# Split chunks, norm scales and gated branches in PSUM banks, and the scalings of the residual between index sums, in a two-block transformer kernel

## The reference

```python
# first block
n = rms_norm(h, norm_mix);  h = h + token_mixers(n, ...)          # recurrence + windowed attention
    merged = sigmoid(gate_r) * y_rec + sigmoid(gate_a) * y_att;  return merged @ w_out
n = rms_norm(h, norm_mem);  mem_n = rms_norm(mem, norm_mem_kv)
h = h + memory_cross_attention(n, mem_n, ...)
n = rms_norm(h, norm_ffn);  h = h + conv_ffn(n, ...)              # (silu(conv(g)) * u) @ w_down
x = rms_norm(h, final_norm)
# second block
h = rmsnorm(x, norm_g)
q_lat, c_kv, k_rope, z_a, q_b, k_b, v_b, z_b, q_idx, k_idx, w_idx, gate_a, gate_b = split(h @ w_in)
q = rmsnorm(q_lat, g_q_lat) @ w_uq;   kv = rmsnorm(c_kv, g_kv_lat) @ w_ukv
y_a = mla_attention(...) * silu(z_a)
y_b = dsa_attention(..., top-k of relu(q_idx . k_idx) weighted by w_idx, rel_bias) * silu(z_b)
merged = sigmoid(gate_a) * (y_a @ w_o_a) + sigmoid(gate_b) * (y_b @ w_o_b)
out = rmsnorm(x + merged @ w_out, final_g)
```

## Time and profile before

| | |
|---|---|
| median of 3 runs | 1524.61 us (1521.25 to 1524.68) |
| the profiled execution | 1524.03 us, span 1522.0 us |
| mean granted clock of TensorE | 0.997 of full speed |
| busy share of the span | PE 95%, PEld 75%, VectorE 68%, GpSimd 55%, ScalarE 30% |
| chain that ended last, by engine | PE 76%, DVE 14%, issue 4%, ACT 3%, POOL 1%, PEld 1% |
| DMA | 127.64 MB read, 6.82 MB written, 88 GB/s over the span |

### The profile page before, as it was taken

How to read it: one execution, slowest core, us unless ns; L and a number is a source line. 1 busy time by engine, 2 the same in 40 slices (tenths; PEclk the granted TensorE clock), 3 DMA queues, 4 the chain that set the end, 5 groups by cost and what they waited for, 6 DMA issues and landing times.

```text
span 1522.0 us, 19925 instructions
## 1 busy us (share of the span) xinstructions
PE 1451.7 (95%) x6948; PEld 1138.0 (75%) x6948; DVE 1035.3 (68%) x1879; ACT 455.3 (30%) x886; POOL 838.7 (55%) x675
## 2 busy tenths in 40 slices
PE   4999999999998899999999999999899999999998
PEld 3777777776777788687888888887677777667886
DVE  6557798687259531588999995335977897686255
ACT  4555441466123111321010101102243334364111
POOL 3534323443565777266777776766645443444663
PEclk9999999999999999999999999999999999999999
DMA  5221111211332333132333333333333531322331
GB/s 204 70 70 42 42 42 49 63 56 56 114 94 84 111 110 103 51 97 84 97 97 97 97 97 99 109 102 128 85 123 98 104 87 47 118 75 99 109 96 57
DMA packets 37018, 135.61 MB, mean 89 GB/s; under 512 B 4296, under 2 KB 4552, under 8 KB 36296
## 3 DMA queue, kind: packets, MB, share of 16 engines
q1 hardware_dynamic: 33264, 121.13, 26.1%
q10 hardware_dynamic: 3672, 13.35, 3.4%
HBM read 127.64 MB, written 6.82 MB: 88 GB/s over the span
## 4 chain that ended last, share of the span: by engine, by line
PE 76%; DVE 14%; issue 4%; ACT 3%; POOL 1%; PEld 1%; DMA 0%; PEldq 0%; ACTq 0%; DVEq 0%; POOLq 0%
PE pair L575 21%; PE pair L577 20%; PE pair L576 20%; PE pair L845 3%; PE pair L873 3%; DVE X L1828 2%; PE pair L857 2%; DVE nL L1666 1%; PE pair L775 1%; DVE rstd L1684 1%; DVE sums L1675 1%; DVE nt L1688 1%; POOL wL L530 1%; DVE lev L1837 1%; DVE hT L2206 1%
## 5 line engine op out<-in xcount | busy, mean ns | idle before, releaser
L530 POOL TENSOR_TENSOR wL<-ring,wH 128x1024 fp32r<-128x1024 f32 x223 | 551.8, 2474 | 18.6
L575 PE MATMUL pair<-nH,wH 128*128 128x512 f32 x1064 | 427.8, 402 | 16.8 <-DVE nL L1666 9.1
L577 PE MATMUL pair<-nH,wL 128*128 128x512 f32 x1064 | 415.8, 391 | 0.0
L576 PE MATMUL pair<-nL,wH 128*128 128x512 f32 x1064 | 415.8, 391 | 0.0
L527 POOL TENSOR_TENSOR tick<-tick 128x1 f32<-128x1 f32 x223 | 56.3, 252 | 645.0 <-PE pair L577 635.6
L575 PEld LDWEIGHTS pair<-nH,wH 128*128 128x128 f32 x1064 | 200.3, 188 | 82.7 <-issue 27.5
L528 POOL TENSOR_SCALAR wH<-ring 128x1024 fp32r<-128x1024 f32 x223 | 239.3, 1073 | 0.0
L577 PEld LDWEIGHTS pair<-nH,wL 128*128 128x128 f32 x1064 | 200.5, 188 | 43.1
L576 PEld LDWEIGHTS pair<-nL,wH 128*128 128x128 f32 x1064 | 200.8, 189 | 40.6 <-issue 1.6
L1513 ACT ACTIVATE sgb<-cv 128x512 f32<-128x512 f32 x22 | 13.9, 634 | 208.9 <-DVE cv L2148 208.9
L575 PE MATMUL pair<-aH,wH 128*128 128x512 f32 x176 | 69.1, 392 | 0.0
(11 more groups left out here) (386 smaller groups left out, 2677.3 us busy)
## 6 DMA issues: line engine op xcount, KB each, us to landing
ring<-stream SPq DMA_DIRECT2D x223, 512.0 KB, 3.6
gvec<-gv ACTq DMA_DIRECT2D x1, 2560.0 KB
hT<-xT SPq DMA_DIRECT2D x4, 512.0 KB, 5.7
x_d<-hT ACTq DMA_DIRECT2D x1, 2048.0 KB, 7.3
toep<-gvec ACTq DMA_DIRECT2D x8, 256.0 KB, 3.5
hT<-x_d ACTq DMA_DIRECT2D x1, 2048.0 KB, 9.6
out<-yo SPq DMA_DIRECT2D x4, 512.0 KB, 4.2
cD<-const_d ACTq DMA_DIRECT2D x1, 1345.0 KB, 5.9
```

The costliest lines, as they stand in the source:

```text
L530: pool.tensor_tensor(wL[:, r % SPL, :], ring[:, r, :], wH[:, r % SPL, :].bitcast(F32), ALU.subtract).then_inc(split_done, 1)
L575: mm(out, a[0], b[0], start=first, stop=False)
L576: mm(out, a[0], b[1], start=False, stop=False)
L577: return mm(out, a[1], b[0], start=False, stop=last)
```

## The change

Nothing that is computed changes, and nothing of what TensorE, GpSimd and SyncE compute or load. What changes is where intermediate values lie, and five places in the order.

- The chunks that are split (`nt`) lie in banks 4 and 5 for ten of the fifteen uses (83 chunks): all but the outputs of the recurrence and the four attentions, where these banks are in use. VectorE writes them there, ScalarE reads the high part's source there, and `low` has one operand in PSUM.
- The inverse deviation of the norms `memory` and `c_kv` goes into bank 2, that of `q_lat` into bank 3. The scale of the final norm (`sums2`) is copied to bank 2 by one new ScalarE instruction, and the chunks 2 to 7 of `mix2` read it there. The other norms keep `rstd`.
- In both merges the gated second branch goes into banks 2 and 3 in place of `addA` and `addD`.
- The eight scalings of the residual leave their place before the inverse of `q_lat`; three stand after index sum 0, three after index sum 1, two after index sum 2. The store of the residual on ScalarE's queue moves from before the first index score's `relu` to after the last one's.
- The sums of the norms of `q_lat` and `c_kv` are each one slot earlier on TensorE.
- The two matmuls of `relb` go to bank 7, before index scores 0 and 1, each with its copy on ScalarE.
- TensorE waits for the last split chunk of `c_kv` before the transposes of `pk` into bank 4.

```diff
+IN_BANKS = {SPLIT[n] + c for n in ("mix", "merged", "memory", "mem", "ffn", "hidden", "mix2", "q_lat", "c_kv", "merged2")
+            for c in range({"hidden": FC, "q_lat": 3, "c_kv": 2}.get(n, DC))}
...
+        def split_at(k, width=S):
+            return (bank(4 + k % 2) if k in IN_BANKS else nt[:, k % 2, :])[:, :width]
...
-            mm(bank(4)[0:8, :], relb[:, :], c_d("onehot", 0, S)[rows, :], start=True, stop=True)
-            mm(bank(5)[0:8, :TOEP - S], relb[:, :], c_d("onehot", S, TOEP)[rows, :], start=True, stop=True).then_inc(gv_done, 1)
             project("q_idx", 0, 1, n_parts, inputs="mix2")
-            project("q_idx", 1, 1, n_parts)
             norm_sum("q_lat")
-            project("small", 0, 1, n_parts)
+            project("q_idx", 1, 1, n_parts)
             norm_sum("c_kv")
+            project("small", 0, 1, n_parts)
             project("z_a", 0, 1, n_parts)
             out_of_bank(pe, FIRST["small"])
-            pe.wait_ge(gv_out, 2)
-            pe.wait_ge(std_made, NORMS.index("final") + 1)
+            pe.wait_ge(nl_made, SPLIT["c_kv"] + 2)
...
             project("z_a", 1, 1, n_parts)
+            pe.wait_ge(std_made, NORMS.index("c_kv") + 1)
+            relative_bias(0, S)
             index_scores(0)
             project("z_a", 2, 1, n_parts)
+            pe.wait_ge(gv_out, 1)
+            relative_bias(S, TOEP)
             index_scores(1)
...
-                A(dst, nt[:, k % 2, :width], ACT.Copy).then_inc(nh_made, 1)
+                A(dst, split_at(k, width), ACT.Copy).then_inc(nh_made, 1)
...
             act.wait_ge(r_made, NORMS.index("final") + 1)
+            A(bank(2), sums2[:, :], ACT.Copy).then_inc(scale_out, 1)
...
-                V.tensor_tensor(lo[:, c, :], nt[:, k % 2, :width], hi[:, c, :].bitcast(F32),
+                V.tensor_tensor(lo[:, c, :], split_at(k, width), hi[:, c, :].bitcast(F32),
                                 ALU.subtract).then_inc(nl_made, 1)
...
+            def scale_of(name):
+                return {"memory": bank(2), "q_lat": bank(3), "c_kv": bank(2)}.get(name, rstd)
...
-                V.reciprocal(rstd[:, :width], std[:, :width]).then_inc(r_made, 1)
+                V.reciprocal(scale_of(name)[:, :width], std[:, :width]).then_inc(r_made, 1)
...
-                    V.tensor_tensor(add[:, c % 2, :], src, g, ALU.mult).then_inc(free, 1)
+                    V.tensor_tensor(bank(2 + c % 2), src, g, ALU.mult).then_inc(free, 1)
                     out_of_bank(dve, FIRST[stage] + 4 * (c // 2) + 2 + c % 2)
-                    V.tensor_tensor(out, add[:, c % 2, :], mt[:, c, :], ALU.add).then_inc(nt_made, 1)
+                    V.tensor_tensor(out, bank(2 + c % 2), mt[:, c, :], ALU.add).then_inc(nt_made, 1)
...
-                                       in1=sums2[:, :], op0=ALU.mult, op1=ALU.mult).then_inc(nt_made, 1)
+                                       in1=bank(2) if c > 1 else sums2[:, :], op0=ALU.mult, op1=ALU.mult).then_inc(nt_made, 1)
...
             inverse("mix2")
-            for c in range(DC):
-                V.scalar_tensor_tensor(out=hT[:, c, :], in0=hT[:, c, :], scalar=vcol("final_norm", c), in1=rstd[:, :],
-                                       op0=ALU.mult, op1=ALU.mult).then_inc(x1_made, 1)
-            dve.wait_ge(x1_made, DC)
             inverse("q_lat")
...
             index_sum(0)
+            final_normed(range(0, 3))
             silu("z_a", [2], za)
             index_sum(1)
+            final_normed(range(3, 6))
             silu("z_a", [3], za)
             index_sum(2)
+            final_normed(range(6, DC))
```

More of the change, by code:

```diff
@@ L343, in build @@
         mnL = place("mnL", [P, DC, MEM], F32R, at=wx0 + 4 * DC * S)
-        addA = place("addA", [P, 2, S])
+        top[0] += 4 * 2 * S
         mk = place("mk", [P, DC, MEM])
@@ L419, in build @@
         assert top[0] <= b0
-        addD = place("addD", [P, 2, S], at=d0)
         mg2L = place("mg2L", [P, DC, S], F32R, at=b0)
@@ L1040, in _, with relative_bias @@
             project("c_kv", 0, 2, u_parts)
-            pe.wait_ge(ld_d, 32)
-            rows = slice(0, REL_BUCKETS)
-            mm(bank(4)[0:8, :], relb[:, :], c_d("onehot", 0, S)[rows, :], start=True, stop=True)
-            mm(bank(5)[0:8, :TOEP - S], relb[:, :], c_d("onehot", S, TOEP)[rows, :], start=True, stop=True).then_inc(gv_done, 1)
+            def relative_bias(a, b):
+                rows = slice(0, REL_BUCKETS)
+                mm(bank(7)[0:8, :b - a], relb[:, :], c_d("onehot", a, b)[rows, :], start=True, stop=True).then_inc(gv_done, 1)
             project("q_idx", 0, 1, n_parts, inputs="mix2")
+            norm_sum("q_lat")
             project("q_idx", 1, 1, n_parts)
-            norm_sum("q_lat")
+            norm_sum("c_kv")
             project("small", 0, 1, n_parts)
-            norm_sum("c_kv")
             project("z_a", 0, 1, n_parts)
             out_of_bank(pe, FIRST["small"])
-            pe.wait_ge(gv_out, 2)
-            pe.wait_ge(std_made, NORMS.index("final") + 1)
+            pe.wait_ge(nl_made, SPLIT["c_kv"] + 2)
+            pe.wait_ge(ld_d, 32)
             for i in range(ST):
@@ L1683, in inverse, with normed @@
                 dve.wait_ge(std_made, i + 1)
-                V.reciprocal(rstd[:, :width], std[:, :width]).then_inc(r_made, 1)
+                V.reciprocal(scale_of(name)[:, :width], std[:, :width]).then_inc(r_made, 1)
                 dve.wait_ge(r_made, i + 1)
-            def normed(out, x, gain, c, width=S):
-                return V.scalar_tensor_tensor(out=out, in0=x[:, c, :], scalar=vcol(gain, c), in1=rstd[:, :width],
+            def normed(name, out, x, gain, c, width=S):
+                return V.scalar_tensor_tensor(out=out, in0=x[:, c, :], scalar=vcol(gain, c), in1=scale_of(name)[:, :width],
                                               op0=ALU.mult, op1=ALU.mult)
@@ L1695, in norm @@
                     beside(c)
-                    normed(open_split(name, c, width), x, gain, c, width).then_inc(nt_made, 1)
+                    normed(name, open_split(name, c, width), x, gain, c, width).then_inc(nt_made, 1)
                     if c:
@@ L2043, in first_branch, with merge @@
                            V.tensor_tensor(mt[:, c, :], src, g, ALU.mult).then_inc(free, 1))
-            def merge(stage, sg, mt, add, name, hi, lo, beside=lambda p: None):
+            def merge(stage, sg, mt, name, hi, lo, beside=lambda p: None):
                 def use(c, src, g, free):
                     out = open_split(name, c)
-                    V.tensor_tensor(add[:, c % 2, :], src, g, ALU.mult).then_inc(free, 1)
+                    V.tensor_tensor(bank(2 + c % 2), src, g, ALU.mult).then_inc(free, 1)
                     out_of_bank(dve, FIRST[stage] + 4 * (c // 2) + 2 + c % 2)
-                    V.tensor_tensor(out, add[:, c % 2, :], mt[:, c, :], ALU.add).then_inc(nt_made, 1)
+                    V.tensor_tensor(out, bank(2 + c % 2), mt[:, c, :], ALU.add).then_inc(nt_made, 1)
                     if c:
@@ L2095, in add_memory @@
                         accumulate("memory", c, MEM)
-            merge("att_mix", sgA, mtA, addA, "merged", mgH, mgL, add_memory)
+            merge("att_mix", sgA, mtA, "merged", mgH, mgL, add_memory)
             inverse("memory", MEM)
@@ L2243, in index_sum, with final_normed @@
                                            op0=ALU.mult, op1=ALU.add).then_inc(t_acc, 1)
+            def final_normed(chunks):
+                for c in chunks:
+                    V.scalar_tensor_tensor(out=hT[:, c, :], in0=hT[:, c, :], scalar=vcol("final_norm", c), in1=rstd[:, :],
+                                           op0=ALU.mult, op1=ALU.mult).then_inc(x1_made, 1)
             index_sum(0)
+            final_normed(range(0, 3))
             silu("z_a", [2], za)
             index_sum(1)
+            final_normed(range(3, 6))
             silu("z_a", [3], za)
             index_sum(2)
+            final_normed(range(6, DC))
             dve.wait_ge(t_acc, 8)
@@ L2295, in _ @@
             barrier()
-            merge("b_mix", sgD, mtD, addD, "merged2", mg2H, mg2L)
+            merge("b_mix", sgD, mtD, "merged2", mg2H, mg2L)
             dve.wait_ge(ld_x1, 16)
```

18 lines of the change are left out of this document (11 added, 7 removed).

## The result

The changed kernel takes **1509.49 us** (median of 4 runs, 1509.26 to 1509.78) against 1524.51 us for the kernel before, measured with it: a ratio of 0.9913, with a 95% interval of 0.9901 to 0.9925. The forecast was 1513.7 us, with a range from 1508 to 1520 and a narrower band from 1511 to 1516.5 us. So the range holds the time and the narrower band does not: 15.0 us were gained where 10.9 were forecast. Run once more, on another occasion, the changed kernel took 1510.50 us (1507.97 to 1511.11) at a ratio of 0.9912 (0.9896 to 0.9928).

A forecast was written before the change was run, and what follows sets the result against it. TensorE, busy 95% of the span, was taken as the bound, waiting on VectorE instructions with two SBUF operands held behind GpSimd's splits. 4.0 + 0.4 + 0.6 + 0 + 5.3 + 0.6 = 10.9 us, from 1524.6 to 1513.7; range 1508 to 1520.

The forecast's parts named there:

- First merge and `mix_out`: First merge to mix_out: four TensorE waits, for low parts and hT, all go; 4.0 us gained, at least 1.8.
- The slots after `mix_out`: Four 256-column slots paced by GpSimd: fewer VectorE pair instructions hold it up; 0.4 us gained, from 0 to 0.9.
- Start of the FFN and its loop: Last nL at the FFN's start comes 0.6 us earlier, at most 1.5; the loop, where TensorE is busy throughout, gains 0.
- Entry: Entry of the second block: waits and a clock fall go, 10.2 us gross, less four prices, net 5.3 us.
- (a): Entry: sums of squares asked for a slot earlier make TensorE wait 1.3 us, from 0 to 2.
- (b): Entry: new wait for the last c_kv split before pk's transposes costs 2.0 us, from 0 to 4.4.
- (c): Entry: relb matmuls now stand between closely following products and cost 1.2 us, not hidden.
- (d): Entry: residual scalings moved between the index sums cost 0.4 us, or 2.5 if one meets a split.
- the 1.7 us of clock: Entry: the granted clock's fall to 0.72 over 6 us behind the wait for sums goes, gaining 1.7 us.
- The write into PSUM: Wherever VectorE writes banks: no extra cost taken; 0.2 us an output would cost 1.6 at the start, 1 more later.
- the free run: Rival: the entry runs freely, (a), (b) and (d) at 0, plus FFN's 1.5 and GpSimd's 0.9; 1508.5 us, chance 0.11.
- the change doesn't do what it says: Rival: GpSimd's split holds VectorE whatever its operands, only the moves count; within 1 us of 1524, chance 0.06.

The follow-up runs named there:

- order-only kernel: The changed kernel with every buffer back in SBUF, the changed order and the wait for c_kv's last split kept: 1526.95 us, ratio 1.0025.
- loop experiment: The changed kernel with the 22 split chunks of the FFN's hidden layer back in SBUF: 1509.63 us, ratio 0.9911.
- banks only: The changed kernel with the entry's old order of scalings and sums put back, the places in banks kept: 1514.97 us, ratio 0.9943.
- the merges: The changed kernel with the gated second branches of both merges back in SBUF: 1511.38 us, ratio 0.9916.
- the reordered entry: The changed kernel with mix2's inverse between the c_kv products, c_kv's root before the copy of small, scalings four and four behind index sums 0 and 1: 1504.76 us.

## Why the prediction came out as it did

**What bounds the kernel and why VectorE was late: right in the main.** The order-only kernel brings the old waits back without any change of order at the merge, and the changed kernel has none of them. All low parts of 128x512 with a PSUM source take 0.68 to 0.69 us, as foreseen. What the prediction says of two SBUF operands is not the whole of it, though. The gain of the norms of `mem` and the FFN has a single input tile, and in SBUF it was held too:

```profile
L2104 DVE TENSOR_SCALAR nt<-hT,vec x16: 475/790/2620, 475.2 to 683.1; 128x512 f32<-128x512 f32 x16
...
L2118 DVE TENSOR_SCALAR pair<-hT,vec x16: 744/754/757, 466.9 to 677.0; 128x512 f32<-128x512 f32 x16
```

The longest, 2.62 us before the change, began at 475.22, 0.11 us behind a weight split of 2.44 us. Into the bank none of the 16 is held. The merges' additions show the converse: with both inputs in SBUF, an output in a bank didn't help.

**First merge and `mix_out`: right in mechanism, 4.0 forecast, 5.05 + 1.50 measured.** Two terms of the sum were short. I added up the waits as the list gives them. A wait also costs the restart: at 459.31 the row says 1.19 us, and TensorE won 1.35 there and 0.12 more one instruction later. The list counts idle time from the end of the last matmul, 0.39 us after its start, while in an unbroken stream the next starts after 0.23: that is the 0.16 between 1.19 and 1.35. The 0.12 comes because the first matmul after a stop is followed at 0.34 us and not at 0.23. Four waits of 3.96 us in all gave 5.05, so 0.27 us apiece beyond what the list says. And I left out the wait for `addA` (0.9 us in two), which the list of before has further down and which this change removes; with its restarts it gave 1.2. Another 0.3 came around the sum at 452.28 us, where the list has no wait; what made it is open.

**The slots after `mix_out`: 0.4 forecast, 0.9 as the upper bound, 1.05 measured.** The mechanism was that a VectorE pair instruction also holds GpSimd up, and that the additions into `sums` take the subtraction's place. They do, but before two subtractions and an accumulation held a GpSimd instruction each, and now one accumulation does. GpSimd's timeline in the changed kernel and before:

```profile
500.55 0.65 POOL L533 TENSOR_TENSOR tick<-tick 128x1 f32<-128x1 f32 x1
501.16 1.04 POOL L534 TENSOR_SCALAR wH<-ring 128x1024 fp32r<-128x1024 f32 x1
...
504.94 0.18 POOL L533 TENSOR_TENSOR tick<-tick 128x1 f32<-128x1 f32 x1
505.10 1.04 POOL L534 TENSOR_SCALAR wH<-ring 128x1024 fp32r<-128x1024 f32 x1
...
505.77 0.64 POOL L527 TENSOR_TENSOR tick<-tick 128x1 f32<-128x1 f32 x1
506.37 1.49 POOL L528 TENSOR_SCALAR wH<-ring 128x1024 fp32r<-128x1024 f32 x1
...
510.58 0.64 POOL L527 TENSOR_TENSOR tick<-tick 128x1 f32<-128x1 f32 x1
511.18 1.05 POOL L528 TENSOR_SCALAR wH<-ring 128x1024 fp32r<-128x1024 f32 x1
```

A free `tick` takes 0.19 us and a free high part 1.05. Before, two ticks took 0.64 and one high part 1.49, after that only one tick: 0.9 us of delay removed, plus a restart.

**Start of the FFN and its loop: right.** 0.57 against 0.6 us, with a wait of 1.08 us for the last `nL`, as named. The loop gave nothing, and VectorE is 46 us less busy in it (some 45 forecast).

**Entry: 5.3 forecast, 5.70 measured, and right in nearly every term.** `qlat` gave 1.31 (its wait of 1.0 and the restarts). `q_idx` 0 starts at 1069.59, another 3.08 us earlier, which is 1.74 + 0.86 + 0.38 + 0.1. Of the prices:

```profile
1082.57 1.12 PE L566 MATMUL pair<-sums,ones 128*128 128x512 f32 x2 [1.03 <-DVE sums L1686]
...
1096.60 0.63 PE L1067 MATMUL pair<-ident,pk 128*128 128x128 f32 x4 [1.99 <-issue]
...
1105.22 1.02 PE L1052 MATMUL pair<-cD,relb 32*8 32x512 f32 x2
1106.17 0.71 PE L1084 MATMUL pair<-ki,qi 32*128 32x256 f32 x8
...
1129.75 1.14 PE L1084 MATMUL pair<-ki,qi 32*128 32x512 f32 x8 [0.26 <-DVE selm L2253]
```

(a) is 1.03 us, where 1.3 was forecast; (b) is 1.99 against 2.0; (c) is 1106.17 - 1105.22 = 0.95 and 0.32 for the second, 1.27 against 1.2; (d) is 0.5 in two waits against 0.4. That they are so near owes something to luck, since each is a difference of two chains of several rows.

One term of this sum, the 1.7 us of clock, is not confirmed. I foresaw a full clock throughout at the entry. The first profile of the changed kernel has that; the second, with the same waits, does not (0.79 over 1092 to 1100 us), nor has that of the loop experiment.

**Merge before `out2`:** 0.86 against 0.6, again the restarts. **The write into PSUM:** taken at nothing, measured at 6 to 8 ns an instruction (L2062 at 0.699 us in the median, where it had 0.692 into SBUF). The one exception is the gain of the norms of `mem` and the FFN, an instruction with a single input tile: it takes 0.744 us at best into PSUM, where its shortest in SBUF was 0.475 but its median 0.790, so the move cost nothing. The Trainium skill, "VectorE: DVE Perf Modes", section "The TRN2 errata", has 62 cycles more for a PSUM source, which gives 65 ns an instruction and, as an estimate, 1.6 us on the path. The trace disagrees: the median of `nL` with a PSUM source is 683 ns, and the shortest one in SBUF was 677.

**Which rival came nearest is not which was right.** At 1509.5 us the time is almost that of the free run (1508.5), yet the free run was defined by (a), (b) and (d) at nothing, and all three are there. Of the 4.2 us between forecast and measurement the trace shows 3.9: 1.5 beside the first merge, 1.05 of restarts, 0.65 of GpSimd's slots, 0.4 at the entry and 0.3 at `out2`. Read from the time alone, the wrong case would have been confirmed. A rival that I priced wrongly is the one in which the change doesn't do what it says: for the moves alone I had said within 1 us of 1524, with a wait for `c_kv` of 3 to 4 us. It was 5.0, and behind it the clock fell as it had before the change (0.72 over 6 us), where I had counted that fall as gained; the kernel was slower than before, clear of noise. That price mattered only to a case with a chance of 0.06, but the case would have been placed on the wrong side.

## What to carry to other kernels

Where VectorE and GpSimd both work out of SBUF, look at the median against the shortest of a line: if it is longer by up to the length of the other engine's instruction, one of two input operands in a free PSUM bank takes the whole delay away, for the additions as well as the subtractions (a bank for the output alone does not), and only where TensorE waits does it count. Price a wait of TensorE as the list's number plus about a quarter of a microsecond, go through the whole list and not its head, and before moving work earlier ask what the shared bank it needs makes the others wait for: here that wait alone turned the same order from a gain of 0.2% into a loss of 0.2%.

## What the runs showed of the hardware

**TensorE's clock falls at the same work in one execution and not in the next.** The granted clock over three stretches (columns as above) in the second run of the changed kernel:

```profile
212.00:220.00 8.00, 5.99 (x20) 1.00 0.22 66
262.00:270.00 8.00, 7.31 (x33) 1.00 0.21 66
1092.00:1100.00 8.00, 6.70 (x19) 0.79 0.32 103
```

and in the first:

```profile
212.00:220.00 8.00, 6.17 (x17) 0.79 0.22 66
262.00:270.00 8.00, 7.57 (x29) 0.79 0.22 66
1092.00:1100.00 8.00, 6.01 (x24) 1.00 0.27 77
```

The program is the same and so are the waits ahead of these places, 2.0 us at 212 and 2.0 at the transposes of `pk`. In the twelve traces of this case the clock falls near 212 in nine, near 264 in six, and at the entry in six, each time to 0.6 to 0.8 on average over 6 to 8 us, partly at the lower level. A fall costs some 1.5 us of the span, and in three of the nine near 212 (banks only, order only, the merges), where it is down to 0.6, twice that:

```profile
212.00:220.00 8.00, 5.97 (x14) 0.60 0.22 66
```

Much of the scatter of every kernel here goes with it: the runs of before in one set go from 1520.2 us at a mean clock of 0.999 to 1526.0 at 0.996. At the entry the four profiles with a wait of 3 to 5 us all have a fall behind it, of the six with waits of 1 to 2 us two have one, and the two with no wait but 0.2 us have none. That is a possible part of the 1.8 us by which the reordered entry beat its trace, though so few profiles don't show it. The fall of 1.7 us that I counted as gained at the entry was gone in the first profile of the changed kernel, but at 212 us one came that the profile of before didn't have.

**The last transfer can differ by 1.5 us.** From ScalarE's last instruction to the end of the span it took 6.2 us in the profile of before and 4.6 to 4.7 in all eleven others. I read nothing of the change into it; the medians of runs are the measure.
